# Two expert tables joined in DRAM, and gathered as pairs of rows in groups of four experts

## The reference, cut to what matters

```python
q = einsum('bsd,de->bse', h, w_q)                      # 8 heads x 256
s1, s2 = q[..., :128] . keys1, q[..., 128:] . keys2     # 128 scores each
v1, i1 = top_k(s1, 16);  v2, i2 = top_k(s2, 16)
vals, c = top_k(v1[..., :, None] + v2[..., None, :], 16)
expert = i1[c // 16] * 128 + i2[c % 16]                 # 8 x 16 = 128 per token
gate = softmax(vals)
act = gelu(einsum('td,ted->te', h, u_tab[expert]))      # 1024-long dot products
out = einsum('te,ted->td', gate * act, v_tab[expert])   # weighted sum of v rows
```

## Time and profile before

| | |
|---|---|
| median of 3 runs | 3343.18 us (3341.9 to 3343.9) |
| the profiled execution, own time | 3344.73 us |
| its span, first to last instruction | 3342.9 us |
| busy: PE, DVE, POOL, ACT | 2809.0, 1849.4, 1216.9, 884.3 us |
| DMA moved | 706.47 MB, of it 536.94 MB by POOL's gathers |
| first and last gather start | 1846.3, 3323.5 us |

### The profile page before, as it was taken

How to read it: one execution, slowest core, us unless ns; L and a number is a source line. 1 busy time by engine, 2 the same in 40 slices (tenths; PEclk the granted TensorE clock), 3 DMA queues, 4 the chain that set the end, 5 groups by cost and what they waited for, 6 DMA issues and landing times. The chain is left out here.

```text
span 3342.9 us, 31046 instructions
## 1 busy us (share of the span) xinstructions
PE 2809.0 (84%) x10832; PEld 1865.1 (56%) x10832; DVE 1849.4 (55%) x3524; ACT 884.3 (26%) x1621; POOL 1216.9 (36%) x1236
## 2 busy tenths in 40 slices
PE   6999999999899999999999786766776667757777
PEld 5888587765677677898778632222332222323323
DVE  4761544244534564556344676656667666757443
ACT  2112322514446564324223211111111111111111
POOL 0000210000202241540001466666666666666665
PEclk7999999999999999999999898878888878878878
DMA  6452123200221123003233799999999999999998
GB/s 235 154 186 88 63 82 96 88 26 1 87 90 63 52 89 119 1 1 115 88 111 110 264 352 370 365 370 390 371 368 364 380 368 386 353 374 382 367 369 312
DMA packets 228772, 706.47 MB, mean 211 GB/s; under 512 B 23188, under 2 KB 25492, under 8 KB 227735
## 3 DMA queue, kind: packets, MB, share of 16 engines
q0 software_dynamic: 147456, 536.94, 41.8%
q1 hardware_dynamic: 81176, 167.76, 14.6%
HBM read 694.13 MB, written 10.49 MB: 211 GB/s over the span
## 5 line engine op out<-in xcount | busy, mean ns | idle before, releaser
L2836 PE MATMUL work_banks<-rows_over_split,sig 128*128 128x512 f32 x1024 | 518.9, 661 | 265.7 <-issue 191.6
L2836 PEld LDWEIGHTS work_banks<-rows_over_split,sig 128*128 128x128 f32 x1024 | 214.6, 212 | 562.0 <-issue 482.3
L219 DVE TENSOR_TENSOR weights_low<-weights_raw,weights_high 128x2048 fp32r<-128x2048 f32 x108 | 250.5, 2320 | 430.4 <-ACT weights_high L214 420.9
L2836 PE MATMUL work_banks<-weights_raw,sig 128*128 128x512 f32 x512 | 266.5, 678 | 155.3 <-issue 90.9
L2928 DVE CUSTOM_DVE_ANT_0 proj_banks<-rows_over_parts,work_banks 128x1024 f32<-128x1024 f32 x256 | 309.1, 1245 | 155.5 <-DMA rows_over_parts<-in_peer_u_dram,eidx 74.6
L277 PE MATMUL proj_banks<-h_low,weights_high 128*128 128x512 f32 x896 | 357.9, 399 | 27.9 <-DVE weights_low L219 9.1
L214 ACT CAST weights_high<-weights_raw 128x2048 fp32r<-128x2048 f32 x108 | 206.0, 1907 | 610.9 <-PE proj_banks L277 582.7
L277 PE MATMUL proj_banks<-h_high,weights_low 128*128 128x512 f32 x896 | 352.7, 394 | 0.0
L277 PE MATMUL proj_banks<-h_high,weights_high 128*128 128x512 f32 x896 | 352.5, 393 | 0.0
L2722 POOL DMA_INDIRECT rows_over_split<-in_peer_v_dram,eidx x256 | 241.6, 944 | 156.2 <-issue 71.9
L2836 PEld LDWEIGHTS work_banks<-weights_raw,sig 128*128 128x128 f32 x512 | 109.3, 219 | 310.5 <-issue 245.3
(11 more groups left out here) (490 smaller groups left out, 4934.5 us busy)
## 6 DMA issues: line engine op xcount, KB each, us to landing
weights_raw<-in_w_in_dram SPq DMA_DIRECT2D x36, 1024.0 KB, 4.9
weights_raw<-in_ret_w_in_dram SPq DMA_DIRECT2D x24, 1024.0 KB, 5.2
ret_gate<-in_mod_w_dram SPq DMA_DIRECT2D x20, 1024.0 KB
weights_raw<-in_fox_w_in_dram SPq DMA_DIRECT2D x16, 1024.0 KB, 5.2
weights_raw<-in_ret_w_out_dram SPq DMA_DIRECT2D x8, 1024.0 KB, 5.2
weights_raw<-in_peer_w_q_dram SPq DMA_DIRECT2D x8, 1024.0 KB, 5.3
ret_v<-in_mod_w_dram SPq DMA_DIRECT2D x4, 1024.0 KB
weights_raw<-in_fox_w_out_dram SPq DMA_DIRECT2D x4, 1024.0 KB, 5.1
```

What stands on the lines that cost most here:

```text
L219: nc.vector.tensor_tensor(wlo[h][:, :, :], raw[h][:, :, :], whi[h][:, :, :].bitcast(F32), ALU.subtract).then_inc(w_split[h], 1)
L2836: last = nc.tensor.matmul(pa[:, half, :], diag[:, s, e, :], v_row(s, e)[:, half * CW:(half + 1) * CW], start=(first and e == 0), stop=(las ...
```

## The change

1. A table `joined` in DRAM, 16384 rows of 8 KB: a row holds an expert's `u` row and behind it its `v` row. It is filled by 128 DMAs from DRAM to DRAM of 1 MB (256 rows of one table), which SP issues one at a time (`join_rows`): one behind each weight load (not in the first 8 chunks of one early stage), and between waits that were added to SP in the attention stages and in the delta rule. `load_chunks` is unrolled for it.
2. One gather (`gather_pair`) fetches 128 rows of 8 KB, u and v of one expert column. 512 gathers are left, each into a buffer of 8 KB per partition that is free when PE has weighed its v half (`v_used`); DVE's dot product frees nothing any more.
3. Groups of GE = 4 columns, 32 a tile; 4 sets of buffers (SETS), so 16 pairs of rows, in the same memory as the 32 single rows before. Gelu, gate and diagonals go by fours; the units of the choice of experts are spread one a group; `add_rows` follows the second group of a tile. PE's program is unrolled.
4. The gathers wait for the whole join (`rows_joined`); the tail's segments are 2 and 2 columns in place of 4, 2 and 2.

```diff
+    def join_rows(sp, pieces=1):
+        for piece in range(state["joined"], min(state["joined"] + pieces, JOIN_PIECES)):
+            rows = slice(piece // 2 * JOIN_ROWS, (piece // 2 + 1) * JOIN_ROWS)
+            table = a["peer_v_2" if piece % 2 else "peer_u_2"][0]
+            sp.dma_start(joined[rows, piece % 2 * D:(piece % 2 + 1) * D], table[rows, :]).then_inc(rows_joined, 16)
+            state["joined"] = piece + 1
...
         for h in range(2):
             sp.wait_ge(w_split[h], g + 1)
             sp.dma_start(raw[h][:, :, :], src(c, h)).then_inc(w_loaded[h], 16)
+            if join:
+                join_rows(sp)
...
-        H, NQ, HK, GE = PEER_HEADS, 2 * PEER_HEADS, PEER_HEADS * TOPK, 8
+        H, NQ, HK, GE = PEER_HEADS, 2 * PEER_HEADS, PEER_HEADS * TOPK, 4
+        PRE = 16
+        SETS = PRE // GE
...
-        def gather_row(to, table, t, k):
+        def gather_pair(to, t, k):
             return nc.gpsimd.indirect_dma_start(
-                out=to, out_offset=None, in_=table,
+                out=to, out_offset=None, in_=joined,
...
-    SEGMENTS = ((0, 4), (4, 6), (6, 8))
+    SEGMENTS = ((0, 2), (2, 4))
...
                     for e in range(GE):
-                        pe.wait_ge(diag_ready, r * (2 * GE) + (t * NG * GE + s * GE + e + 1))
-                        pe.wait_ge(v_loaded[s][e], r * 16 + 16 * (t * NG // 2 + 1))
+                        pe.wait_ge(diag_ready, (t * NG + g) * GE + e + 1)
...
+                            if t_of < TT:
+                                if j % 4 < 2:
+                                    top_keys(t_of, h, j % 4)
+                                elif j % 4 == 2:
+                                    top_pairs(h)
+                                else:
+                                    experts(t_of, h, 1)
+                            weights_of(t, g)
...
-                    for g in range(2, LAST):
-                        gather(u_tab, g, g % 2, dot_done, u_loaded)
-                        gather(v_tab, g, g % 2, v_used, v_loaded)
+                    pool.wait_ge(rows_joined, 16 * JOIN_PIECES)
+                    for g in range(SETS, LAST + 1):
...
+                        for e in range(GE):
+                            pool.wait_ge(v_used, g * GE + (e + 1))
+                            gather_pair(pair(g % SETS, e), g // NG, (g % NG) * GE + e
+                                        ).then_inc(pair_loaded[g % SETS][e], 16)
```

More of the change, by code:

```diff
@@ L58 @@
 NEG = -1.0e30
+JOIN_PIECES = 128
+JOIN_ROWS = PEER_KEYS * PEER_KEYS * 2 // JOIN_PIECES
 C_IDENT = 0
@@ L195, in load @@
             sp.dma_start(raw[h][:, :, :], src(c, h)).then_inc(w_loaded[h], 16)
+            if join:
+                join_rows(sp)
     def load_chunks(sp, src, n, then=None):
         g0 = state["g"]
[L200 to L205, removed]
+        for c in range(1, n):
+            load(sp, src, c, g0 + c)
         if then is not None:
@@ L2892, in _ @@
                             pe.wait_ge(y_added, t)
[L2893 to L2899, removed]
+                        for g in range(NG):
+                            weigh(pe, t, g)
                 @block.vector
@@ L3023, in _, with diagonals @@
                                        pa[:, t, :].rearrange("p (f c) -> p f c", c=P)).then_inc(sc_ready, 1)
+                    def diagonals(n_of, lo=0, hi=GE):
+                        for e in range(lo, hi):
+                            nc.scalar.activation(diag[:, n_of % SETS, e, :], ident, ACT.Copy,
+                                                 scale=coef[:, n_of % SETS, e:e + 1]).then_inc(diag_ready, 1)
                     for t in range(TT):
@@ L3075, in gather @@
-                    def gather(table, g, s, used, loaded, rows=(0, GE)):
-                        t, first = g // NG, (g % NG) * GE
-                        if table is u_tab and g == NG // 4:
+                    pool.wait_ge(rows_joined, 16 * JOIN_PIECES)
+                    freed = {(0, 2): (x_put, 16), (0, 4): (w_split[0], state["g"] + n + 1),
+                             (0, 5): (w_split[1], state["g"] + n + 1), (0, 6): (first_used, state["g"] + n + 1),
+                             (1, 2): (tile_full[3], state["g"] + n + 1), (1, 6): (s_full, 4 * n)}
@@ L3079, in gather @@
+                    for g in range(SETS):
+                        for e in range(GE):
+                            if divmod(g * GE + e, 8) in freed:
+                                pool.wait_ge(*freed[divmod(g * GE + e, 8)])
+                            gather_pair(pair(g, e), 0, g * GE + e).then_inc(pair_loaded[g][e], 16)
+                    for g in range(SETS, LAST + 1):
+                        if g == NG // 4:
                             pool.wait_ge(eidx_ready, 2)
-                        elif table is u_tab and g == NG // 2:
+                        elif g == NG // 2:
@@ L3081, in gather @@
                             pool.wait_ge(eidx_ready, 3)
-                        elif table is u_tab and g > NG // 2 and g % 2 == 0:
-                            pool.wait_ge(eidx_ready, 3 + g // 2 - NG // 2 + 1)
-                        for e in range(*rows):
-                            pool.wait_ge(used, g * GE + (e + 1))
-                            gather_row(u_row(s, e) if table is u_tab else v_row(s, e), table, t, first + e
-                                       ).then_inc(loaded[s][e], 16)
@@ L3089, in _ @@
-                    for g in range(2, LAST):
-                        gather(u_tab, g, g % 2, dot_done, u_loaded)
-                        gather(v_tab, g, g % 2, v_used, v_loaded)
-                    for rows in SEGMENTS:
-                        gather(u_tab, LAST, LAST % 2, dot_done, u_loaded, rows)
-                        gather(v_tab, LAST, LAST % 2, v_used, v_loaded, rows)
+                        elif g > NG // 2 and g % 4 == 0:
+                            pool.wait_ge(eidx_ready, 3 + g // 4 - NG // 4 + 1)
```

163 lines of the change are left out of this document (76 added, 87 removed).

## The result

The changed kernel takes 3209.25 us (median of 4 runs, 3208.2 to 3211.26) beside 3343.54 for the kernel before: 0.9596 of it, 95% interval 0.9579 to 0.9612. 3196 was forecast. The profiled execution took 3211.26 us, with a span of 3209.5.

The account below looks back on a forecast made before the run. POOL's issue and waits were taken as the bound. Start 1913, 496 pairs x 2.50 (1240), 3 for landing, 12 for the end, 20 for dips and 8 for the join made 3196 us; own range 3140 to 3266, 8-in-10 range 3140 to 3358.

Parts of the forecast that it names:

- The bound: Gather stage: POOL's issue, 1.24 us a gather, together with some 225 us of waits; DMA at 0.95 busy follows.
- What the waits are: Gather stage: counts arrive late, 18 us for POOL, while many small gathers are in flight, not because DMA is full.
- These increments crowd the others out: Gather stage: inferred cause of late counts, about 13 gather increments each microsecond, falling to 6.4 with half the gathers.
- The rate: Gather stage: rows of 8 KB move at 420 GB/s, so a pair of rows for a column takes 2.50 us.
- The memory's limit: Rival, gather stage: memory limits DMA to its mean of 366 GB/s, 2.87 us a pair, total 3357; chance 0.07.
- The ring and PE: Gather stage: sixteen pairs last 40 us against a buffer's life of 20 to 27; PE takes 2.1 us a column.
- The rival in which PE's late counts hold both halves: Gather stage: each pair waits for PE's late count, mean 2.84 us a pair, total 3365; chance 0.12.
- The end: After the last landing: 12 us, 6 for the last two columns' work and 6 for the sum and store.
- The join: Stages before the gathers: 128 copies of 1 MB cost 8 us, with 0 and 30 as ends.
- the first gather within 10 us of 1846: Start of the gather stage: a sign that would show the forecast right.
- Loads come 12 us apart: Stages with copies: spacing of the loads that copies lie behind, from 16 loads in 193 us, used in costing the join.

Follow-up runs that it names:

- The rows of 2 KB: The kernel before, with every gather behind the first 32 fetching 2 KB rows in place of 4 KB, still 1024 gathers: 3343.89 us, 0.9994.
- groups of four and of eight: Four is the changed kernel, 3209.25 us; eight is the changed kernel with groups of eight columns in two sets of buffers, 3212.04 us, 0.9575 of the kernel before.
- two gathers: The changed kernel with each pair fetched by two gathers of 4 KB rows from the two tables, 1024 gathers: 3368.94 us, 1.0043 of the kernel before.
- the copies alone: The kernel before with the 128 copies of the change added, its 1024 gathers still from the two tables: 3368.38 us, 1.0048.
- twelve copies moved: The changed kernel with 12 copies put behind later weight loads: 3193.99 us, 0.9514 of the kernel before on the first chip; 3191.19 us, 0.9943 on the second.

## Why the prediction was right, and where its reasons were not

**The bound.** Right on the first chip, and more so than the argument had it: POOL's issue and its waits. The rows of 2 KB show it directly. The gain is that of the waits. Two gathers take POOL 2 x 1.24 = 2.48 us, and DMA drains a pair in 2.48; with no late counts there is nothing for the pairing to win, and on the second chip it won 3 us. The prediction didn't ask whether another chip would have the waits.

**What the waits are.** That counts are late with many gathers, and not because DMA is full, stood on the chip where it could be seen (188 GB/s, 3343.9 us). "These increments crowd the others out" fell: as many increments from SP's DMAs did nothing (3211.9). What brought the lateness back was gathers issued by POOL, with next to no bytes. How POOL's issuing delays the counts of DVE and PE is open, and so is why the second chip doesn't show it. So this step was right in what it forecast, that halving the gathers removes the late counts, and wrong in the mechanism that it gave.

**The rate.** A pair was put at 2.50 us. Full windows give 422 to 424 GB/s, 2.48 us. 496 pairs with dips and the last landing were 1240 + 20 + 3 = 1263 us in the sum; from the first gather of the second round to the last pair's dot product it is 3197.1 - 1933.9 = 1263.2. That it meets to the us is luck in part: 496 x 2.48 is 1230, so landing and dips took 33 where 23 were put. The memory's limit is out: 419 over 1000 us against the mean of 366. The 358 GB/s of the Trainium skill ("DMA: Bandwidth & Descriptors", section "Where 436 GB/s comes from") doesn't bind these gathers of a core that runs alone; the measured 419 decides, and it is near the other figure that the prediction quotes, about 425 for such a core.

**The ring and PE.** The reserve was there, with groups of four and of eight: both held 419 GB/s. PE was put at 2.1 us a column; it is 779 us for some 400 columns, 1.95, at a clock of 0.91. The rival in which PE's late counts hold both halves did not come: with half the gathers no late count shows. Where the number of gathers stayed and both halves waited for PE (two gathers), it cost nothing over the copies alone either.

**The end.** 12 us were forecast from the last landing; it is 3209.5 - 3197.1 = 12.4.

**The join: the term that was mis-sized.** 8 us were taken, with 30 as the upper end; 21.2 came. This is the whole miss of 13, and the sign "the first gather within 10 us of 1846" failed. 16 us are the copies': on the second chip the first gather comes at 1862.5 with the change and at 1846.3 with twelve copies moved, so the other 116 copies cost nothing that shows. These 16 us arise where loads that somebody waits for come behind copies, at two places. `w_ba`, 64 KB, in the kernel after:

```profile
L1962 SPq DMA_DIRECT2D w_ba<-in_w_in_dram x1: 417/417/417, 1132.2 to 1132.2; - x1
...
  DMA w_ba<-in_w_in_dram: 15.5, 1
...
DMA to landing us min/median/max: 17.1/17.1/17.1
```

Eleven copies went out in the 32 us ahead of it, two for each of the last heads, and it landed 17.1 us after its issue. With the copies moved it lands after 3.4 and 3.1. What this costs is read from ACT's splits of the weights on both sides of it, before (L214) and after (L225):

```profile
1125.85 1.90 ACT L214 CAST weights_high<-weights_raw 128x2048 fp32r<-128x2048 f32 x1 [4.00 <-PEq L1735]
...
1146.71 1.89 ACT L214 CAST weights_high<-weights_raw 128x2048 fp32r<-128x2048 f32 x1
```
```profile
1131.88 1.91 ACT L225 CAST weights_high<-weights_raw 128x2048 fp32r<-128x2048 f32 x1 [4.17 <-PEq L1752]
...
1161.98 1.90 ACT L225 CAST weights_high<-weights_raw 128x2048 fp32r<-128x2048 f32 x1
```

30.1 us in place of 20.9: 9.2 are lost. The second place is the gates, where a tile of 2 MB that was stored away (z) is read back behind copies. DVE's row there, in the kernel after:

```profile
DVE gdn_qkv L2617 <- DMA gdn_qkv<-z_away: 4.9, 1, 4.9
```

The splits on both sides start 18.0 us apart (1590.4 and 1608.3), and 11.5 in the kernel before (1573.8 and 1585.2): 6.5 more. Both losses are there in the second chip's profile of the change (9.2 and 6.6), and in neither kernel with the copies moved.

What is left of the 21.2 varies from one profile to the next. Most of it is the clock granted to TensorE in one stretch: 0.57 from 725 to 737 us in the profile of the change (the window above), that is mostly the lower of its two levels (1.2 GHz), where the kernel before and the change on the second chip have 1.00 (2.4 GHz). PE's idle time ahead of it is the same in both profiles (2.3 us, near 720.6), and DMA is at 0.01. ACT's first record behind it starts at 746.5 us before and at 751.3 after. The other kernels' profiles have 0.57 to 1.00 there; what sets it is not shown.

The step that failed is thus the pacing of the copies. "Loads come 12 us apart" was read from a stage of weight loads (by its own rows it is 12.9); in the last heads of the stick-breaking stage the copies come 3 us apart, and nothing paces them.

## What to carry to other kernels

A DMA share near 1 does not make DMA the bound: look for the engine that issues, and ask what happens with half the bytes. An indirect gather cost POOL 1.24 to 1.25 us whatever its length (2, 4 or 8 KB rows), so longer rows cost the issuing engine nothing, up to the rate of DMA (here 2.48 us for a pair). Copies to join tables can be nearly free, if they are kept away from small loads that somebody waits for. A gain that rests on late counts should be measured on more than one chip before it is believed: this one was 4% on one and 0.1% on the other (0.6% with the twelve copies moved).

## What the runs showed of the hardware

While POOL issues gathers on end, DVE's counts can be late by 1.5 to 5 us for tens of us, at 188 GB/s as at 370, and POOL can see a count of PE 18 us and 25 us (rows of 2 KB) after PE's records have it. Two kernels with nearly the same number of extra packets and increments, one from SP and one from POOL, differ by 142 us. A queue of gathers of 8 KB rows held 419 GB/s over 1000 us. A load of 64 KB landed 17.1 us after its issue behind eleven copies of 1 MB, and 3.1 to 3.4 us without them. The same kernel took 3345 to 3355 us on one chip and 3210 on another, while the changed one took 3207 and 3209 us where it was timed.
